# Two norms of one residual: one transposition of x times its power, the gain vectors applied as columns in the hi/lo split

## The reference, cut to what matters

```python
def rms_norm_2(x, g):
    xf = x.astype(jnp.float32)
    y = xf * lax.rsqrt(jnp.mean(xf * xf, axis=-1, keepdims=True) + EPS)
    return (y * g.astype(jnp.float32)).astype(x.dtype)
...
k, v = jnp.split(rms_norm_2(x, kv_norm_g) @ w_kv, 2, axis=-1)
...
h = rms_norm_2(x, b_norm_g)
q, z = jnp.split(h @ w_qz, 2, axis=-1)
```

## Time and profile before

| | us |
|---|---|
| three runs | 859.15, 858.82, 858.85 |
| median | 858.85 |
| span of the profiled execution, first to last instruction | 857.6 |
| PE busy | 850.0 (99%) |
| PEld busy | 739.9 (86%) |
| DVE busy | 640.9 (75%) |
| ACT busy | 526.8 (61%) |
| POOL busy | 61.3 (7%) |

### The profile page before, as it was taken

One profiled execution on the slowest core, in us unless ns is written; L12 is line 12 of the kernel. 1 busy time (PEld: TensorE's weight loads), 2 busy tenths in 40 slices (PEclk: granted clock), 3 DMA queues, 4 the chain that ended last, 5 costly groups with the idle time before them and its releaser, 6 DMA issues.

```text
span 857.6 us, 12037 instructions
## 1 busy us (share of the span) xinstructions
PE 850.0 (99%) x4791; PEld 739.9 (86%) x4791; DVE 640.9 (75%) x798; ACT 526.8 (61%) x740; POOL 61.3 (7%) x68
## 2 busy tenths in 40 slices
PE   9999999999999999999999999999999999999997
PEld 8988888888889898888888888888888898888885
DVE  5899999987698656765466468759777777877873
ACT  6777777756575544653554457548666665576772
POOL 0022222310000000000000000100000001000001
PEclk9999999999999999999999999999999999999999
DMA  8976555554644655576456545686666655853501
GB/s 271 311 272 201 183 196 197 189 162 156 207 148 140 205 195 174 172 231 233 149 169 231 190 148 194 200 284 217 213 192 197 217 177 168 263 176 110 191 1 50
DMA packets 124183, 162.47 MB, mean 189 GB/s; under 512 B 3928, under 2 KB 111200, under 8 KB 124128
## 3 DMA queue, kind: packets, MB, share of 16 engines
q1 hardware_dynamic: 122320, 154.89, 54.3%
q0 software_dynamic: 1504, 6.29, 2.3%
q10 hardware_dynamic: 304, 0.53, 0.2%
HBM read 160.65 MB, written 1.05 MB: 189 GB/s over the span
## 4 chain that ended last, share of the span: by engine, by line
PE 98%; DVE 1%; issue 0%; POOL 0%; POOLq 0%; DVEq 0%
PE pAcc L453 23%; PE pG L397 9%; PE pU L397 9%; PE pAcc L397 7%; PE pR L397 5%; PE pG L400 5%; PE pU L400 4%; PE pM L397 4%; PE pAcc L400 3%; PE pR L400 2%; PE pAcc L431 2%; PE pAcc L433 2%; PE pAcc L432 2%; PE pM L400 2%; PE pG L516 1%; PE pM L433 1%
## 5 line engine op out<-in xcount | busy, mean ns | idle before, releaser
L331 DVE TENSOR_TENSOR lo<-raw,hi 128x2048 fp32r<-128x2048 f32 x131 | 298.5, 2288 | 53.0 <-ACT hi L326 51.6
L326 ACT ACTIVATE hi<-raw 128x2048 fp32r<-128x2048 f32 x140 | 265.8, 1908 | 19.1 <-PE pAcc L433 5.6
L397 PE MATMUL pG<-xT,hi 128*128 128x512 f32 x336 | 83.8, 391 | 0.2 <-DVE stage_a L1846 0.2
L397 PE MATMUL pU<-xT,hi 128*128 128x512 f32 x320 | 80.2, 392 | 0.0
L453 PE MATMUL pAcc<-hi,h_hi 128*128 128x512 f32 x240 | 74.8, 393 | 0.0
L453 PE MATMUL pAcc<-lo,h_hi 128*128 128x512 f32 x240 | 74.2, 390 | 0.0
L453 PE MATMUL pAcc<-hi,h_lo 128*128 128x512 f32 x240 | 74.0, 390 | 0.0
L397 PEld LDWEIGHTS pG<-xT,hi 128*128 128x128 f32 x336 | 62.1, 188 | 13.4 <-issue 1.0
L1142 ACT ACTIVATE h_hi<-h 128x512 fp32r<-128x512 f32 x28 | 17.8, 635 | 80.1 <-PE pAcc L453 74.3
L397 PEld LDWEIGHTS pU<-xT,hi 128*128 128x128 f32 x320 | 57.5, 189 | 10.3
L1667 DVE TENSOR_TENSOR h_lo<-h,h_hi 128x512 fp32r<-128x512 f32 x28 | 19.3, 688 | 46.1 <-ACT h_hi L1142 46.1
(11 more groups left out here) (521 smaller groups left out, 1651.4 us busy)
## 6 DMA issues: line engine op xcount, KB each, us to landing
raw<-in_a_w_in SPq DMA_DIRECT2D x24, 1024.0 KB, 5.3
raw<-in_ffn_wd SPq DMA_DIRECT2D x22, 1024.0 KB, 5.4
raw<-in_ffn_wg SPq DMA_DIRECT2D x21, 1024.0 KB, 5.2
raw<-in_ffn_wu SPq DMA_DIRECT2D x21, 1024.0 KB, 5.9
raw<-in_w_in SPq DMA_DIRECT2D x16, 1024.0 KB, 5.5
raw<-in_a_w_out SPq DMA_DIRECT2D x8, 1024.0 KB, 4.8
raw<-in_w_kv SPq DMA_DIRECT2D x8, 1024.0 KB, 5.4
raw<-in_b_w_qz SPq DMA_DIRECT2D x8, 1024.0 KB, 5.5
```

What stands on the lines that cost most here:

```text
L326: act.activation(HI[n % NHL][:, :], RAW[n % NRAW][:, :], ACT.Copy).then_inc(S["hi"], 1)
L331: dve.tensor_tensor(LO[n % NHL][:, :], RAW[n % NRAW][:, :], HI[n % NHL][:, :].bitcast(f32), ALU.subtract).then_inc(S["lo"], 1)
L397: pe.matmul(v3(bank[:, :], 2), wh[:, k, w], x4[:, :, k, :], start=(k == 0), stop=False, skip_group_check=True)
```

## The change

The key/value and query norm are no longer written as two sets of rows. `rows_plain` writes x * power once (tensor_scalar, without gain), TensorE transposes it once (q = 4), and the same four banks G, U, R, ACC0 are split twice: `xk_hi`/`xk_lo` with norm 0 into XK, and with norm 1 into XT. Each split multiplies by the gain, which lies along partitions there, as a scale column [128, 1] (tile CG, 16 columns in GAIN[1]: 8 feature groups by 2 norms). Since each feature group has a column of its own, a bank takes four instructions of 128x128 on either engine where it took one of 128x512.

Gone: the 16 transposes of the query norm on TensorE, four row instructions on VectorE, and two broadcast loads of 1024 gains, which one load of 128x16 replaces. k0 now waits for xt_lo at 24, that is for the whole second split, as its banks G and U are the ones that are split. The norm's gain load for the end waits on the second split.

```diff
-            transposes(pe, 5, 0)
-            transposes(pe, 5, 1)
...
-            wide(("chunk", "k", 0), WK[0], [(S["xt_lo"], 16 + 4)] * 2, XK_ALL)
+            wide(("chunk", "k", 0), WK[0], [(S["xt_lo"], 24)] * 2, XK_ALL)
...
+        CG = GAIN[1][:, 0:2 * KD]
+        def gain_of(norm, b, k):
+            c = KD * norm + 4 * (b % 2) + k
+            return CG[:, c:c + 1]
+        def xk_hi(act, norm, x, b):
+            act.wait_ge(S["xt_ps"], 16 + b + 1)
+            act.wait_ge(S["gain1"], 16 * 3)
+            for k in range(4):
+                end = act.activation(xt_dst(x[0], b)[:, k, :], xt_bank(4, b)[:, k * P:(k + 1) * P], ACT.Copy,
+                                     scale=gain_of(norm, b, k))
+            end.then_inc(S["xt_hi"], 1)
+        def xk_lo(dve, norm, x, b):
+            dve.wait_ge(S["xt_hi"], 16 + 4 * norm + b + 1)
+            for k in range(4):
+                end = dve.scalar_tensor_tensor(out=xt_dst(x[1], b)[:, k, :], in0=xt_bank(4, b)[:, k * P:(k + 1) * P],
+                                               scalar=gain_of(norm, b, k), in1=xt_dst(x[0], b)[:, k, :].bitcast(f32),
+                                               op0=ALU.mult, op1=ALU.subtract)
+            end.then_inc(S["xt_lo"], 1)
+        def rows_plain(dve, g, t):
...
+            for n in range(2):
+                dve.tensor_scalar(XN[:, half_row(t, n)], X[:, half_row(t, n)], ST[:, c:c + 1], None,
+                                  ALU.mult).then_inc(S["xn"], 1)
...
             for b in range(4):
-                xt_hi(act, 5, XT, b)
+                xk_hi(act, 1, XT, b)
...
-            for t in range(NT):
-                dve.wait_ge(S["xt_ps"], 16 + 2 * t + 2)
-                rows(dve, 6, t, XN, rstd_of=5)
             lo(dve, n + 3)
             for b in range(4):
-                xt_lo(dve, 5, XT, b)
+                xk_lo(dve, 1, XT, b)
...
-                    load_gain(sp, 5)
-                    load_gain(sp, 6)
+                    sp.wait_ge(S["xn"], rows_done(3, 1))
+                    sp.dma_start(CG, T["chunk_gains"]).then_inc(S["gain1"], 16)
```

More of the change, by code:

```diff
@@ L80 @@
 UNITS = [(0, 0), (0, 1), (1, 0), (1, 1), (2, 0), (2, 1), (4, 0), (4, 1), (3, 0), (3, 1),
-         (5, 0), (5, 1), (6, 0), (6, 1), (7, 0), (7, 1)]
+         (5, 0), (5, 1), (7, 0), (7, 1)]
 RS_COL = {("norm", g, t): (32 + 2 * g + t, 1) for g in (0, 1) for t in range(NT)}
@@ L88 @@
 RS_ORDER = list(RS_COL)
-GAINS = ["ffn1_norm", "mix_norm", "ffn2_norm", "final_norm", "a_norm_g_2", "kv_norm_g_2", "b_norm_g_2",
-         "final_norm_g_2"]
+GAINS = ["ffn1_norm", "mix_norm", "ffn2_norm", "final_norm", "a_norm_g_2", None, None, "final_norm_g_2"]
 def rows_done(g, t, half=1):
@@ L97, in squares_done @@
 def squares_done(g, t):
-    return 2 * [u for u in UNITS if u[0] != 6].index((g, t)) + 2
+    return 2 * UNITS.index((g, t)) + 2
 SEMS = {
@@ L245, in build @@
         ACC = [ctx.enter_context(nc.psum_tensor(f"pAcc{i}", [P, 512], f32)) for i in range(4)]
-        XBANK, XBANK_M, XBANK_B = (G, U, M, R), (G, U, R, ACC[0]), (ACC[2], ACC[3], R, ACC[0])
+        XBANK, XBANK_M = (G, U, M, R), (G, U, R, ACC[0])
         RB = (ACC[0][:, 0:P], ACC[3][:, 0:P])
@@ L360, in load_gain @@
             w = w if len(w.shape) == 1 else w[0]
-            if n > 1:
+            if n == 7:
+                sp.wait_ge(S["xt_lo"], 24)
+            elif n > 1:
                 sp.wait_ge(S["xn"], rows_done(n - 2, 1))
@@ L494, in xt_bank @@
         def xt_bank(q, b):
-            return (XBANK_B if q == 5 else XBANK_M if q in (1, 4) else XBANK)[b]
+            return (XBANK_M if q in (1, 4) else XBANK)[b]
         def transposes(pe, q, t):
@@ L1072, in power_first, with rows @@
                                ALU.pow).then_inc(S["rsqrt"], 1)
-        def rows(dve, g, t, dst, rstd_of=None):
-            what = ("norm", g if rstd_of is None else rstd_of, t)
+        def rows(dve, g, t, dst):
+            what = ("norm", g, t)
             c = RS_COL[what][0]
@@ L1099, in xt_lo @@
                               ALU.subtract).then_inc(S["xt_lo"], 1)
+        CG = GAIN[1][:, 0:2 * KD]
[17 more added lines that the diff above has]
+        def rows_plain(dve, g, t):
+            what = ("norm", g, t)
+            c = RS_COL[what][0]
+            dve.wait_ge(S["rsqrt"], RS_ORDER.index(what) + 1)
+            for n in range(2):
+                dve.tensor_scalar(XN[:, half_row(t, n)], X[:, half_row(t, n)], ST[:, c:c + 1], None,
+                                  ALU.mult).then_inc(S["xn"], 1)
         def xf(b):
@@ L1174, in act_turn @@
                 hi(act, n + 2 + t)
-                xt_hi(act, q, x, 2 * t)
-                xt_hi(act, q, x, 2 * t + 1)
+                for b in (2 * t, 2 * t + 1):
+                    if q == 4:
+                        xk_hi(act, 0, x, b)
+                    else:
+                        xt_hi(act, q, x, b)
         def wide_act(act, b, banks, dst, f, scale=1.0):
@@ L1669, in dve_turn, with x_rows, x_lo @@
         def dve_turn(dve, r, g, q, ph, scale, x, n):
+            def x_rows(t):
+                if q == 4:
+                    rows_plain(dve, g, t)
+                else:
+                    rows(dve, g, t, XN)
+            def x_lo(b):
+                if q == 4:
+                    xk_lo(dve, 0, x, b)
+                else:
+                    xt_lo(dve, q, x, b)
             lo_half(dve, n + 1, 0)
@@ L1676, in dve_turn @@
             variance(dve, g, 0)
-            rows(dve, g, 0, XN)
+            x_rows(0)
             dve.wait_ge(S["acc_end"], 3 * r + 3)
             add_acc(dve, 1, 0, scale)
-            xt_lo(dve, q, x, 0)
-            xt_lo(dve, q, x, 1)
+            x_lo(0)
+            x_lo(1)
             dve.wait_ge(S["used"], NTH[ph, CONTRACT[ph], COUNT[ph] - 1] + 1)
@@ L1684, in dve_turn @@
             variance(dve, g, 1)
-            rows(dve, g, 1, XN)
+            x_rows(1)
             lo_half(dve, n + 2, 0)
-            xt_lo(dve, q, x, 2)
-            xt_lo(dve, q, x, 3)
+            x_lo(2)
+            x_lo(3)
             lo_half(dve, n + 2, 1)
@@ L2688 @@
     arrays["a_par"] = np.concatenate(parts, axis=1)
+    gains = [arrays.pop(name).reshape(KD, P) for name in ("kv_norm_g_2", "b_norm_g_2")]
+    arrays["chunk_gains"] = np.ascontiguousarray(np.concatenate(gains).T)
     nc = bacc.Bacc("TRN2", target_bir_lowering=False, num_devices=1)
```

## The result

The changed kernel takes 869.77 us, median of 4 runs (868.45 to 871.06), against 858.88 us before (858.82 to 859.15): ratio 1.0122, 95% interval 1.0111 to 1.0134 (the quotient of the two medians is 1.0127). It is 1.2% slower, where 870.0 us was forecast. Its profiled execution has a span of 868.0 us (857.6 before), and that run took 869.8. The runs of one kernel tend to lie in two groups 1.6 to 1.8 us apart: of 18 later runs of the kernel before, ten took 858.47 to 859.28 and eight 860.35 to 861.23.

What follows compares the result with a forecast made beforehand. TensorE, busy 850.0 of 857.6 us, was taken to bound the kernel. Span 857.6 + 8.65 (k0's wait) + 2.5 (clock) = 868.75, plus 1.25, gave 870.0 us; range 866.0 to 872.5.

Steps and rivals of the forecast that it cites:

- The new wait: At k0, waiting for XT's last lo: start 8.65 us later, including the turn's 2.0 and the 1.67 of transposes gained.
- a bank of 1.14 us: Four 128x128 instructions with a gain column: 1.14 us a bank, starts 1.04 (ScalarE) and 1.06 (VectorE) apart.
- The turn inside it: First split, at the turn into chunked attention: first v block 1.0 us later, tile 1 2.0 us later in all.
- The lo of bank R: VectorE's first split in the turn: ends at 727.91 instead of 725.91, releasing tile 1.
- the step from there to TensorE: From the end of a lo to the first matmul needing it: 0.24 to 0.29 us, read in the turn.
- The clock: In TensorE's 8.3 us rest before k0: falls from 2.4 to 1.2 GHz, costing 2.5 us, bounds 2.2 to 4.6.
- The sum: Whole kernel: 857.6 + 8.65 + 2.5 = 868.75 of span, plus 1.25, giving 870.0 us, 1.3% slower.
- 1.25: Whole kernel: microseconds by which the median time was taken to exceed the profiled span.
- The clock did not hold: Rival on the rest before k0: clock does not fall or is back at once, 867.5 us; chance 0.10.
- the short instructions were not cheap: Rival on both splits: short column instructions cost little beyond width, k0 +4.8, 866.15 us (863.65 if clock holds); chance 0.09.
- The other side: Rival at k0: second split done before TensorE gets there, only the removed transposes (1.67) count, 857.2 us; chance 0.03.
- As said, it made next to no odds: Tile 1's rows in the turn: even if no faster, bank R's transposes find the first half, the second comes hardly later.

Runs made afterwards that it cites:

- ratio kernel: Changed kernel with the key/value gain back in the rows, first split whole, second split multiplying by the quotient of gains: 867.13 us, ratio 1.0092.
- the one with whole banks and plain rows: Changed kernel with each bank split by one 128x512 instruction on either engine, gains left out, for timing only: 866.86 us, ratio 1.0083.
- filled kernels: Changed kernel with 66 or 33 extra identity matmuls on TensorE before k0: 873.98 us (1.0169) with 66, 867.70 us (1.0103) with 33.
- early split: Changed kernel with the second split moved ahead of hi and v on ScalarE and of q0's lo on VectorE: 859.74 us, ratio 1.0006.
- two banks: Changed kernel with k0 waiting for the second split of banks G and U only (xt_lo at 22): 866.90 us, ratio 1.0086.

## Why the prediction was right

- **The new wait** (+8.65 said, +8.24 found; the rest in it 8.3 said, 7.93 found). Its parts are shown one by one: the wait behind hi and v, 4.15 to 4.17; the cutting of banks, 1.57; the column, 2.52. The last two were taken together, from runs of other instructions in the trace: a bank of 1.14 us was 1.12 to 1.24 on ScalarE and 1.12 to 1.13 on VectorE, with starts 1.00 and 1.04 apart (1.04 and 1.06 said).
- **The turn inside it** (+2.0 said, +1.70 found; the first v block late by 0.84 instead of 1.0). The lo of bank R ends where it was said to, 10.24 us after the first transposes (10.30 said). What was misread is the step from there to TensorE, taken as 0.24 to 0.29 us from places where TensorE was not waiting: before the change it was still in another instruction until it reached the first v block, as this row's stretch shows.

```profile
719.64 0.39 PE L453 MATMUL pAcc<-hi,h_lo_last 128*128 128x512 f32 x1
```

  Where it does wait, the step is 0.05 us (727.23 to 727.28) to 0.14 (740.80 to 740.94). That makes 0.24 of the 0.30 at tile 1, and 0.13 more at k0. The ratio kernel (8.60 to tile 1) and the one with whole banks and plain rows (8.62) show that all of the turn's delay comes from the first split.
- **The clock** (+2.5 said, +2.78 found). That it would fall was read from one place, two microseconds of rest at the end; the filled kernels show that it is the rest. The size lay within its bounds of 2.2 to 4.6, in part by luck: in the five other kernels with a rest of 3.90 us or more it was 1.55 to 2.31, in four of them below the lower bound, and for the very same rest 1.59. A rest's length alone does not give this term.
- **The sum** was closer than its terms. The two main ones came to 11.02 where 11.15 was said. The profiled run was 0.62 ahead before the turn, and 1.8 us lay around its span where 1.25 had been taken. The 1.25 was a misreading: in every execution whose span and time are both known 1.76 to 1.94 lie between them, so the span of 857.6 belongs to a slower execution than the three that gave the median. These two nearly cancel, and neither belongs to the change.
- **The rivals.** The clock did not hold; the short instructions were not cheap, though without the column they come near that case (k0 +5.72, +4.8 said for it). The other side is real but needs another kernel: it took the early split, the whole first split and the shorter wait to get the 1.67 us that the transposes were worth, and 857.2 us is what that rival's sum gave.
- **Not foreseen:** how the rows without gain would go. VectorE did the two of tile 0 in 0.88 us and those of tile 1 in 1.47. As said, it made next to no odds: tile 1's first transposes started on time, those of the second half row 0.08 us later.

## What to carry to other kernels

Where two operands come from one PSUM bank, the second split is no longer free to be late: look at what stands ahead of it in each queue that runs in order, and put it into that engine's idle time before removing the work that covered it. In a kernel bound by TensorE, price a new wait twice, by its length and by the slow matmuls behind it (1.55 to 2.78 us here, for rests of 3.90 us and more). A gain column makes one wide instruction into several short ones with a scalar operand, about double the time here; keep it off the step that is waited for first, and use a quotient of gains if a first operand can be had whole.

## What the runs showed of the hardware

- The clock may fall after the rest has ended. With a rest of 3.90 us it was 1.00 up to 737, where k0 begins, and 0.50 from 739; the mean of 741 to 743 is 0.87, so it was back near 741.5.
- After rests of equal length, 7.93 us, the clock stayed at 0.50 for 6.1 us of k0 in the changed kernel and for 3.5 in the ratio kernel. What sets the moments of fall and return was not tried. The spread of a kernel's runs is no measure of it: the changed kernel's four runs spread over 2.6 us (868.45 to 871.06), but so do 18 of the kernel before (858.47 to 861.23), whose clock does not fall there.
- The plain tensor_scalar of 128x512 from SBUF has 481 to 487 ns, and one of the four 1068:

```profile
L1133 DVE TENSOR_SCALAR xn<-residual,stats x4: 481/487/1068, 715.7 to 723.7; 128x512 f32<-128x512 f32 x4
```

  (min, median, max). The long one starts at 723.7, while GpSimd issues the relative bias's load. In the two banks and early split kernels it is the same one, 1069 and 1072 ns. That GpSimd holds something VectorE needs in this form was not tried.
- 33 float32 matmuls of 128x128 appear as 66 and take 7.53 us: 0.23 us each, twice what one record takes.
